# Seven half-width products for two gate tiles in a two-block transformer kernel

## The reference, cut to what matters

```python
def second_block(x, ...):
    for l in range(DEPTH):                      # DEPTH = 2
        h = rmsnorm_2(x, pre_norm_g[l])
        proj = h @ w_in[l]
        (u, v, z_a, c_q, c_kv, k_rope, z_b, x_c, z_c, g_a, g_b, g_c) = jnp.split(proj, cuts, axis=-1)
        y_a = gmlp_spatial(u, v, ...) * jax.nn.silu(z_a)
        y_b = mla_attention(c_q, c_kv, k_rope, ...) * jax.nn.silu(z_b)
        y_c = rg_lru(x_c, ...) * jax.nn.silu(z_c)
        merged = (jax.nn.sigmoid(g_a) * (y_a @ w_proj_a[l])
                  + jax.nn.sigmoid(g_b) * (y_b @ w_proj_b[l])
                  + jax.nn.sigmoid(g_c) * (y_c @ w_proj_c[l]))
        x = x + rmsnorm_2(merged @ w_out[l], post_norm_g[l])
    return x
```

## Time and profile before

| | |
|---|---|
| median of 3 runs | 3152.33 us (3152.31 to 3152.98) |
| the profiled execution's span | 3150.8 us |
| around the span, to the median | 1.5 us |
| TensorE busy | 3140.4 us |
| DVE, ScalarE, GpSimd busy | 1859.9, 1258.6, 394.9 us |
| granted TensorE clock | 1.000 |

### The profile page before, as it was taken

The page is one execution under the profiler, slowest core; times in us unless marked ns, Lnnn a source line. Parts: engine busy times, 40 slices in busy tenths (PEclk is TensorE's granted clock), DMA queues, the critical chain, the costliest instruction groups (busy, mean ns, idle before and its releaser), DMA issues.

```text
span 3150.8 us, 36896 instructions
## 1 busy us (share of the span) xinstructions
PE 3140.4 (100%) x14840; PEld 2628.4 (83%) x14840; DVE 1859.9 (59%) x2504; ACT 1258.6 (40%) x1889; POOL 394.9 (13%) x287
## 2 busy tenths in 40 slices
PE   9999999999999999999999999999999999999999
PEld 8888888888888888888888888888888888888887
DVE  6876456665687655665557642447656754344754
ACT  4323334434433334443445422226635442223742
POOL 1201112110020121112012000110011100011001
PEclk9999999999999999999999999999999999999999
DMA  4332323235442223222642232223332222323432
GB/s 170 116 101 94 101 94 108 100 123 191 149 121 96 97 89 113 96 98 97 204 144 88 78 102 92 89 94 118 124 132 73 82 94 96 98 87 96 138 99 102
DMA packets 105354, 345.42 MB, mean 110 GB/s; under 512 B 13824, under 2 KB 14080, under 8 KB 104416
## 3 DMA queue, kind: packets, MB, share of 16 engines
q1 hardware_dynamic: 101856, 328.47, 32.1%
q0 software_dynamic: 3184, 14.06, 1.3%
q10 hardware_dynamic: 144, 0.52, 0.1%
HBM read 324.65 MB, written 2.10 MB: 104 GB/s over the span
## 4 chain that ended last, share of the span: by engine, by line
PE 96%; DVE 3%; ACT 1%; DMA 0%; SPq 0%; issue 0%; POOL 0%; POOLq 0%
PE ps L520 94%; DVE r L1484 1%; PE ps L611 1%; DVE wl L1474 1%; PE ps L852 0%; DVE f L1489 0%; SPq L2261 0%; DVE f L1552 0%; DMA X<-x_in 0%; DMA f<-f 0%; DVE r L1900 0%; DVE f L1722 0%; ACT wh L982 0%; ACT f L1308 0%; DVE sm L1921 0%; PE ps L564 0%
## 5 line engine op out<-in xcount | busy, mean ns | idle before, releaser
L520 PE MATMUL ps<-h,wh 128*128 128x512 f32 (+1 forms) x5824 | 1695.3, 375 | 0.7 <-DVE wl L1474 0.3
L520 PEld LDWEIGHTS ps<-h,wh 128*128 128x128 f32 x5824 | 1063.4, 188 | 200.1 <-issue 3.4
L520 PE MATMUL ps<-h,wl 128*128 128x512 f32 (+1 forms) x2912 | 1091.2, 375 | 0.0
L1474 DVE TENSOR_TENSOR wl<-raw,wh 128x1024 fp32r<-128x1024 f32 (+1 forms) x583 | 739.1, 1280 | 294.9 <-ACT wh L982 293.7
L982 ACT CAST wh<-raw 128x1024 fp32r<-128x1024 f32 (+2 forms) x596 | 592.3, 1006 | 685.9 <-PE ps L520 684.7
L520 PEld LDWEIGHTS ps<-h,wl 128*128 128x128 f32 x2912 | 547.1, 188 | 98.9
L520 PE MATMUL ps<-r,wh 128*128 128x512 f32 x1536 | 473.4, 389 | 0.9 <-DVE r L1484 0.5
L520 PEld LDWEIGHTS ps<-r,wh 128*128 128x128 f32 x1536 | 288.1, 188 | 62.2 <-issue 2.1
L1074 ACT CAST r<-f 128x512 fp32r<-128x512 f32 x194 | 119.8, 621 | 517.1 <-DVE f L1820 149.0
L520 PE MATMUL ps<-r,wl 128*128 128x512 f32 x792 | 304.3, 389 | 0.0
L520 PE MATMUL ps<-wh,r 128*128 128x512 f32 x960 | 302.4, 390 | 0.3
(11 more groups left out here) (160 smaller groups left out, 2133.5 us busy)
## 6 DMA issues: line engine op xcount, KB each, us to landing
raw<-wst SPq DMA_DIRECT2D x544, 512.0 KB, 3.3
raw<-wst SPq DMA_DIRECT2D x48, 320.0 KB, 3.0
r<-r SPq DMA_DIRECT2D x64, 128.0 KB, 2.3
f<-gains POOLq DMA_DIRECT2D x6, 1024.0 KB, 5.2
raw<-wst SPq DMA_DIRECT2D x20, 256.0 KB, 3.0
f<-f SPq DMA_DIRECT2D x72, 64.0 KB, 2.0
f<-tab POOLq DMA_DIRECT2D x16, 256.0 KB, 4.4
X<-x_in SPq DMA_DIRECT2D x4, 512.0 KB, 8.2
```

What stands on the lines that cost most here:

```text
L520: return e.matmul(o, a, b, start=start, stop=stop, skip_group_check=True)
L1474: e.tensor_tensor(l[:, 0:WIDTH[c]], raw[:, c % NRAW, 0:WIDTH[c]], h[:, 0:WIDTH[c]].bitcast(F32), ALU.subtract).then_inc(*lo_cut.up(("lo", c)))
```

## The change

In the second block 16 pairs of gate tiles (two in b, three each in a and c, in both layers) are made by Strassen's scheme in Winograd's form. A pair is a 2 x 2 product: two column tiles of the weights by two halves of k, times two halves of k by two halves of the positions. Each of the seven products has 4 blocks k and 256 positions.

- GpSimd forms the four combined weights of a pair (`sums`) from its two raw chunks, and once in a layer the four combined h (`mix`, eleven sums of 128 x 1024, in front of the attention's end on its queue). Seven half chunks are cut in place of two whole.
- The combined h need room: X is doubled, x is stored to HBM at the start of the layer (`save_rows`) and read back at its end (`rows_back`, ahead of the gains on GpSimd's queue).
- The products accumulate in three banks. ScalarE copies four intermediate sums out of PSUM in time for TensorE to add to the same bank, DVE makes three sums of halves, then the sigmoids follow.
- The order of chunks, cuts, gate buffers and layer normalisations is written anew; outside the pairs LA = 2 stays. The low weights lie without the further 16 words. GpSimd's descriptor space is cut to 1024.

The core of the diff:

```diff
-AHEAD = {0: 1, 1: 1, 2: 1, "b": 1, "a": 1, "c": 2}
+AHEAD = {0: 1, 1: 1, 2: 1}
+PAIR_J = {"b": (3, 5), "a": (2, 4, 6), "c": (2, 4, 6)}
...
+            if nm != "b":
+                gate(0)
+                gate(1)
+            for n, j in enumerate(PAIR_J[nm]):
+                gate(j)
+                gate(j + 1)
+                product(2 * n)
+                product(2 * n + 1)
+            if nm == "b":
+                gate(7)
+            for j in range(2 * len(PAIR_J[nm]), 8):
+                product(j)
...
+def released(r):
+    c = RAW_OF.index(r) if r in RAW_OF else RAW_OF.index(r - 1)
+    if c not in PART:
+        return (("lo", c),)
+    return ("sums", CHUNKS[c][0][:-2], 3), ("lo", c + 2)
+def sums_free(name, q):
+    L, nm, j = int(name[0]), name[6], int(name[8])
+    if j != PAIR_J[nm][0]:
+        return ("lo", NAME[f"{name[:8]}{j - 2}*{q}"])
+    return {"b": ("done", ("ob", L, 7)), "a": ("gated", L, "b", 7), "c": ("done", ("ri", L, 9))}[nm]
...
-        put(t, f"{L}/prb_0", [[("layer_norm", L, i)] for i in range(4)])
...
+              "b": lambda L: ("done", ("ob", L, 7)), "a": lambda L: ("gated", L, "b", 7), "c": lambda L: ("c_lo", L, 9)}
+STEPS = {b: lambda one, two, after: (one, two, after and after + "*0", after and after + "*1") for b in "ba"}
+STEPS["c"] = lambda one, two, after: (one + "+", "", two, after + "*1" if after else two + "+")
...
+            def two_tiles(L, name, between):
+                c = NAME[f"{name}*0"]
+                first, second, third = (take((name, i)) for i in "abc")
+                product(first, name, 0, 0, quarter(0, 0), True).then_inc(*group_done.up(("done", (name, "p1"))))
+                for m in "1643":
+                    w.wait_ge(*at("mixed_lo", L, m))
+                product(second, name, 0, 1, combined("1"), True).then_inc(*group_done.up(("done", (name, "n5")), ("closed", c)))
+                product(third, name, 1, 0, quarter(0, 1), True, True).then_inc(*group_done.up(("done", (name, "p2"))))
+                w.wait_ge(*at("copied", name, "p1"))
+                product(first, name, 1, 1, combined("6")).then_inc(*group_done.up(("done", (name, "u2")), ("closed", c + 1)))
+                w.wait_ge(*at("copied", name, "n5"))
+                product(second, name, 2, 0, combined("4"), False, True).then_inc(*group_done.up(("done", (name, "p3"))))
+                between(0)
+                w.wait_ge(*at("copied", name, "u2"))
+                product(first, name, 2, 1, combined("3")).then_inc(*group_done.up(("done", (name, "u3")), ("closed", c + 2)))
+                between(1)
+                w.wait_ge(*at("copied", name, "u3"))
+                product(first, name, 3, 0, quarter(1, 1), False, True).then_inc(
+                    *group_done.up(("done", (name, "c21")), ("closed", c + 3)))
+                between(2)
...
+                for n, j in enumerate(PAIR_J[b]):
+                    two_tiles(L, f"{L}/gate{b}_{j}", lambda i: some(2 * n + (i > 1), (whole[:cut], whole[cut:], whole)[i]))
+                if b == "b":
+                    tile(f"{L}/gateb_7", xs)
+                for j in range(2 * len(PAIR_J[b]), 8):
+                    some(j, whole)
```

ScalarE's program of a pair and of a group (the copies `kept` and the sigmoids):

```diff
+                w.wait_ge(*at(*gate_free(L, b, j)))
+                kept(g0[:, lo], "a", "p1")
+                kept(g0[:, up], "b", "n5")
+                first()
...
+                if b == "b":
+                    for j in (1, 2):
+                        gate_sigmoid(L, b, j)
+                else:
+                    for j in range(2):
+                        slot(f"{L}/gate{b}_{j}")
+                        gate_sigmoid(L, b, j)
...
+                for n, j in enumerate(PAIR_J[b]):
...
+                    to(f"{name}*3")
```

DVE's program (`gated` multiplies gate and product):

```diff
+            def two_gates(L, b, j, n, first, second, then):
...
+                e.tensor_tensor(g1[:, up], g0[:, up], g1[:, up], ALU.subtract).then_inc(*dve_tile.up(("c22", name)))
+                then(0)
+                gated(L, b, 2 * n)
+                then(1)
+                gated(L, b, 2 * n + 1)
...
+                    if after:
+                        to(f"{after}*2")
+                    if n:
+                        merged((2 * n - 2, 2 * n - 1))
+                    if b == "b":
+                        small_step("layer_norm", L, n)
+                if b == "b":
+                    slot(f"{L}/gateb_7")
+                for j in range(2 * len(PAIR_J[b]), 8):
+                    slot(f"{L}/pr{b}_{j}{more}")
+                    if j == 6:
+                        merged((4, 5))
+                    if b == "b" and j in (4, 5):
+                        small_step("layer_norm", L, j - 2)
+                    gated(L, b, j)
+                merged((6, 7))
```

GpSimd's (the waits of `mix` are left out but for the order of its sums):

```diff
+                for q, (a, b) in enumerate(((one[:, 0:S], two[:, 0:S]), (t[0], two[:, S:2 * S]), (two[:, 0:S], two[:, S:2 * S]),
+                                            (t[1], one[:, S:2 * S]))):
+                    w.wait_ge(*at(*sums_free(name, q)))
...
+                step(A, h_quarter(0, 1, 0), h_quarter(0, 1, 1), ALU.subtract, ("mix", L, "1", 0))
+                step(N, h_quarter(1, 1, 0), h_quarter(1, 1, 1), ALU.subtract, ("mix", L, "1", 1))
+                step(A, A, N, ALU.add, ("mixed", L, "1"), seen("1", 0), seen("1", 1))
...
                 for r in (4, 0, 1, 2, 3):
                     roped(L, r, 59)
+                mix(L, L + 2)
...
+                for b in "ac":
+                    for j in PAIR_J[b]:
+                        sums(f"{L}/gate{b}_{j}")
+                        if j > 2:
+                            add_gated(L, b, (j - 4, j - 3))
+                    add_gated(L, b, (4, 5, 6, 7))
```

More of the change, by code:

```diff
@@ L122, in proj, with gate, product @@
         def proj(nm, w, nk, b):
[L123 to L128, removed]
+            def gate(j):
+                one(f"gate{nm}_", D2["gate"] + 1024 * b, j)
+            def product(j):
                 if nk == 8:
@@ L683, in after, with gate_proj @@
                 early_second(B)
-            def gate_proj(L, b, g, p, ys, ready, first=0, kind="one"):
+            def gate_proj(L, b, g, p, ys, ready):
                 xs = pair(0, 8, 8)
                 n = AHEAD[b]
-                if first == 0:
-                    for j in range(n):
-                        tile(f"{L}/gate{g}_{j}", xs)
+                for j in range(n):
+                    tile(f"{L}/gate{g}_{j}", xs)
                 for j in range(8):
-                    if 1 < j <= first:
-                        banks.let_go(f"{L}/gate{g}_{j - 1}")
-                    if first <= j + n < 8:
+                    if j + n < 8:
@@ new lines, in gate_proj, with product @@
+                    last = group(o, h, l, [(j % 2 * 4 + k) * P for k in range(4)], ys)
+                    closes = (("closed", NAME[name]),) if j % 2 else ()
+                    last.then_inc(*group_done.up(("done", key), *closes))
+            def product(o, name, q, second, xs, start=False, stop=False):
+                c = NAME[f"{name}*{q}"]
+                h, l = split_at(c)
+                w.wait_ge(*at("lo", c, second))
+                for k, (xh, xl) in enumerate(xs):
+                    col = second * S + k * P
+                    last = three(o[:, halves(0)], h[:, col:col + P], l[:, col:col + P], xh, xl, start and k == 0, stop and k == 3)
+                return last
@@ L702, in gate_proj, with gate_proj2, some @@
+            def gate_proj2(L, b, ys, ready):
+                xs = pair(0, 8, 8)
+                def some(j, ks, halved=False):
+                    key, n = ("pr", L, b, j), 8 if len(ys) == 8 else 5
+                    for k0 in range(ks[0] - ks[0] % n, ks[-1] + 1, n):
+                        name = f"{L}/pr{b}_{j}" + ("+" if k0 else "")
                         h, l = weights(name)
-                        o = take(key)
-                        for k in range(4):
+                        o = take(key) if ks[0] == 0 and k0 == 0 else bank(key)
+                        part = [k for k in ks if k0 <= k < k0 + n]
+                        for k in part:
@@ new lines, in some @@
+                        ends = (("done", key),) if part[-1] == len(ys) - 1 else ()
+                        ends += (("closed", NAME[name]),) if part[-1] == k0 + n - 1 else ()
+                        if ends:
+                            last.then_inc(*group_done.up(*ends))
+                whole = range(len(ys))
+                cut = len(ys) // 2
+                if b == "b":
+                    banks.let_go(f"{L}/gateb_1")
+                    banks.let_go(f"{L}/gateb_2")
+                else:
+                    for j in range(2):
+                        tile(f"{L}/gate{b}_{j}", xs)
```

395 lines of the change are left out of this document (286 added, 109 removed).

## The result

The changed kernel takes **3225.05 us** (median of 4 runs, 3224.7 to 3225.76) against 3152.32 us of before (4 runs): ratio 1.0231, 95% interval 1.0216 to 1.0245, 72.7 us slower. The profiled execution's span is 3224.0 us, 73.2 above that of the earlier trace rows.

A forecast was written before the change was run, and what follows sets the result against it. TensorE, busy 100%, was taken to bound the kernel. 3150.8 us less 15.8 saved, plus 66.8 of stalls and 6 for the clock, gave 3207.8; with 1.5 for the median, 3209 us, range 3170 to 3235.

The forecast's parts named there:

- The saving: TensorE in the 16 pairs: 84 half-width matmuls at 117.8 ns replace 48 full-width ones, 15.8 us less.
- The seven places: Stalls of TensorE at seven seams of each layer, behind other engines' queues: 33.4 us a layer, 66.8 in all.
- end of c: Behind c's last pair, TensorE waits for VectorE's merged-tile low parts, a GpSimd sum's turn and the 640-wide cut: 4.4 us.
- start of b: At b's first pair, the third PSUM bank is free only after a late sigmoid on ScalarE: 3.0 us.
- first pair of c: ScalarE's first copy waits for the recurrence, 7.2 us; GpSimd's sums push VectorE's scans some 3.1: 10.3 us.
- attention: At the start of attention, GpSimd's 1024-wide sums take turns with VectorE's last low parts: 5.0 us.
- The clock: TensorE's granted clock halves in four long stalls, 1.5 us each: 6 us, with 20 as upper end.
- Rival C: The clock falls in every long stall, or the inner steps wait for sums: 3225 to 3245 us; chance 8%.
- A: TensorE stays covered, waits under 7.9 us a layer, so only the saving is left: 3136.5 us; chance 9%.
- B: Only queue order counts; GpSimd's turns and the bank cost nothing: 3178 us; chance 18%.
- D: Half products run at full price, or gain and waits meet: within 6.3 us of before; chance 3%.
- At nothing: Work costed at zero as covered: half casts and cuts, sums, raw buffers, combined x, x to HBM and back.

The follow-up runs named there:

- e6: The changed kernel with five reorderings together: those of e1, e3, e4, e5, and product 6 cut earlier at the ends of a and c; 3153.5 us.
- e11: The kernel before with only the low weights moved to multiples of 1024 words, without the further 16; 3153.0 us.
- e5: The changed kernel with ScalarE's sigmoids of gate tiles b 1 and 2 moved right behind its last attention step; 3215.3 us.
- e3: The changed kernel with another gate buffer ring for c, and copies and cuts of c's first pair moved earlier; 3216.7 us.
- e12: The e6 kernel with GpSimd's four sums of c's first pair left out, cuts reading raw half weights instead; 3152.95 us.
- e10: The changed kernel with the edits of e1, e4, e5 and e9, and product 6 cut earlier at the ends of a and c; 3145.0 us.
- e7: The e6 kernel with three more chunks cut earlier around the first pair of c; 3157.7 us.
- e4: The changed kernel with GpSimd's eleven sums of the combined x started only after the second head's scores; 3211.9 us.
- e8: The kernel before, with eight pauses of TensorE made by short GpSimd sums and nothing of the change; 3194.4 us.
- e1: The changed kernel with two cuts and each normalisation in group b moved ahead of the last pair's gate products; 3206.5 us.
- e9: The changed kernel with gate tiles 2 and 3 of c made at full width in the old order, 14 pairs left; 3205.9 us.

## Why the prediction was right, and where it was off

Forecast 3209 us, range 3170 to 3235, slower with 0.88; measured 3225.05, 16 above the forecast and inside the range. The gaps were right in their causes and came out 4 us smaller than summed, the pace took 2 us more, and the clock 18.5.

- **The saving** was right. Two rows of TensorE's timeline inside a pair of a, with 45 half-width matmuls from the first to the second, and the row of the next block k:

```profile
2074.07 0.40 PE L620 MATMUL ps<-mixed,wh 128*128 128x256 f32 x2
2079.37 0.63 PE L620 MATMUL ps<-r,wh 128*128 128x512 f32 x2
2080.07 0.62 PE L620 MATMUL ps<-r,wh 128*128 128x512 f32 x2
```

  That is 5.30 us, 117.8 ns each. What a pair saves in the whole is a little less: in e6 the stretch from the attention to the spatial mix, with two pairs, is 1.83 us shorter than before, 0.92 a pair against 0.985. Full-width matmuls next to half-width ones are dearer: the three matmuls from the second row to the third take 0.70 us where three cost 0.68. Over 16 pairs that is 1.0 us, and with the boundary stretches of e11 (1.2 us there) it is about the 2 us left in the ledger. (The low weights lost not only the 16 words that the prediction names but also the 64 between slots.) The reason given for 117.8 ns, that half-width work right behind full-width work shows the slower rate, was not borne out: in the trace of before the slower and the faster stretches at the boundaries all follow 128-wide matmuls. The number held all the same.
- **The seven places** were right, all seven, by place and by releaser. Predicted and measured in us, layer 2 (layer 3 is the same within 0.5): end of a 2.2 and 2.17; end of b 6.7 and 6.72; second pair of b 1.8 and 1.80; end of c 4.4 and 4.04; start of b 3.0 and 3.44; first pair of c 10.3 and 1.66 + 7.82 = 9.48; attention 5.0 and 3.75 more than the 1.2 of before. The sum was put at 66.8 us and the distances give 63.2. At the end of c GpSimd's gated sum did stand between DVE's two low parts (2.35 us for the two in place of 1.29).
- **The clock** is the step that failed. I wrote "I take 1.5 for each of the four, 6 us", with 20 as the upper end, since the only fall in the trace of before came 3.9 us after the last matmul. The falls came behind every gap of 3.4 us or more, ten of them, and cost 24.5 us, 1.4 to 4.2 each. This term is 18.5 us too small, more than the whole error of 16 us. The number was wrong (ten, not four) and so was the price. The upper end, 20, was too low as well. (The upper ends of the places, 7.5, 4 and 3.3, add up to 37.1 a layer and not 36.6; that moves the 3230 by 1.)
- **Rival C** (the clock falls in every long stall, 3225 to 3245, 8%) is what happened, at its lower end. The range held it because it reached half into C, not because the forecast had the clock right. I gave it too little: five places were within 1 us of the 3.9 or above, and one observed delay is not a threshold. **A** fell: the waits are four times the 7.9 us a layer. **B** fell: the turns with GpSimd are real (8.38 for 4.21 us at the attention), and so is the bank (e5). **D** fell with the pace.
- **At nothing** stood the half casts and cuts inside a group, the buffers, the x from HBM and the combined x beside the heads. None of them shows a wait: outside the seven places no gap over 0.4 us is in the second block of the changed kernel. GpSimd is busy 143 us more, 150 forecast.
- **Not foreseen**: that the first pair of c has three late items, not one (e3, e6, e12), and that the kernel can be mended (e10).

## What to carry to other kernels

A scheme that takes matmuls away from a kernel whose TensorE never waits is paid for in the order of the other queues: here 15.8 us were saved and 62.5 of gaps and 24.5 of half clock were bought with them, nearly all of it at the ends and starts of groups; inside a group only the second pair of b waits, 1.8 us a layer. Look for the item that stands ahead of the next cut at each such seam, move it back to where the old order had it, and leave the scheme out where several late items meet: here that gave 8.5 us (e10 against e6), while one more try at the order lost 4 (e7), by an item that itself had to wait. Where dense matmuls follow, as here, count a gap of TensorE over some 3 us at its length and some 2.4 us more, the mean of these ten; what one costs is 0.47 us for each us of matmuls at the lower clock.

## What the runs showed of the hardware

- The granted clock fell to half behind every gap of TensorE of 2.8 us or more in these traces but one (3.44 us, in e4), with or without other work beside it (e8), and behind neither of 1.3 us in e8. In between it goes both ways: behind the same gap of 2.17 us never in the changed kernel, twice in e1, once each in e3, e4 and e9, and once behind 1.2 us in e4. The Trainium skill (TensorE: Matmul & The Clock Gate, Why this matters for your kernels) warns of idle gaps between bursts; the runs agree, and show falls behind single gaps of 1.2 and 2.17 us as well.
- What a fall costs does not grow with the gap: 1.4 to 4.2 us of slower matmuls in the changed kernel, 1.4 to 3.0 in e8. Part of the half-clock stretch can lie in the gap and costs nothing: 4.6 of 10.24 us behind the gap of 7.82 us. A series of short gaps can do it as well: 1.46 and 2.36 us close to each other had one in both layers of e3 and none in e6's trace.
- Four DVE instructions of 64 x 512 took 4.21 us beside one GpSimd sum of 128 x 512 (e4 and the earlier trace rows) and 8.38 when two sums of 128 x 1024 followed it, which themselves took 2.84 where 2.4 was their time later in e4: here DVE paid more in such turns than GpSimd.
- Two stretches of half-width matmuls, at 825 and 1623 us, ran faster with the low weights in slots 1088 words apart and 16 words further in them than with both taken away: 113.3 ns against 117.8 in the first (e11). Other stretches ran at 117.8 with them too.
